# Two quarters of a value projection cut into token pieces: one between attention score steps, one around the transposes of the softmax maxima

## The reference

```
proj = h @ w_in                                   # 1024 -> qc,kc,vc (512 each), qd,kd,vd (768 each)
oc   = stick_breaking(qc, kc, vc)                 # 8 heads of 64
# for each dilation group g in (1, 4, 16), 4 heads of 64:
logits = q k^T / 8 + bias ; masked outside the window
m = max(logits); p = exp(logits - m); den = sum(p)
o_g = p v / den ; lse_g = m + log(den)
od   = sum_g softmax_g(lse_g) * o_g
y    = concat(oc, od) @ w_out
```

## Time and profile before

| | us |
|---|---|
| median of 3 executions | 1382.39 |
| lowest, highest | 1375.46, 1383.12 |
| the profiled execution, its own time | 1371.74 |
| its span, first to last instruction | 1369.9 |
| PE busy in it | 1327.1 (97%) |
| DVE, ACT, POOL busy | 608.6, 466.0, 508.2 |

### The profile page before, as it was taken

One profiled execution on the slowest core, in us unless ns is written; L12 is line 12 of the kernel. 1 busy time (PEld: TensorE's weight loads), 2 busy tenths in 40 slices (PEclk: granted clock), 3 DMA queues, 4 the chain that ended last, 5 costly groups with the idle time before them and its releaser, 6 DMA issues.

```text
span 1369.9 us, 17106 instructions
## 1 busy us (share of the span) xinstructions
PE 1327.1 (97%) x6566; PEld 1107.0 (81%) x6566; DVE 608.6 (44%) x826; ACT 466.0 (34%) x655; POOL 508.2 (37%) x209
## 2 busy tenths in 40 slices
PE   7999999999999999999999999998999999999996
PEld 6778877788888888888888777888888888887885
DVE  5489657767534343401747333367681110100005
ACT  3443353543232322112423433317342322322122
POOL 0343322324453544544343312221154444444444
PEclk9999999999999999999999999989999999999998
DMA  9963437523545465843235311111133322234312
GB/s 335 175 154 100 178 123 139 184 78 123 203 164 204 164 219 179 199 125 106 113 135 184 116 51 62 62 59 56 50 98 95 104 92 92 93 106 138 92 62 62
DMA packets 93539, 173.82 MB, mean 127 GB/s; under 512 B 15735, under 2 KB 61959, under 8 KB 93356
## 3 DMA queue, kind: packets, MB, share of 16 engines
q1 hardware_dynamic: 90344, 169.63, 40.6%
q10 hardware_dynamic: 3140, 3.43, 0.9%
HBM read 170.87 MB, written 4.52 MB: 128 GB/s over the span
## 4 chain that ended last, share of the span: by engine, by line
PE 83%; issue 9%; POOL 4%; DVE 2%; ACT 1%; DMA 0%; POOLq 0%; SPq 0%; DVEq 0%; ACTq 0%
PE ps L1128 15%; PE ps L1129 14%; PE ps L1130 14%; PE ps L1160 5%; PE ps L1162 5%; PE ps L1161 5%; POOL w_lo L697 3%; PE ps L1297 2%; PE ps L1298 2%; PE ps L1299 2%; PE ps L1657 1%; PE ps L1685 1%; PE ps L1311 1%; PE ps L1265 1%; PE ps L1267 1%
## 5 line engine op out<-in xcount | busy, mean ns | idle before, releaser
L697 POOL TENSOR_TENSOR w_lo<-raw,w_hi 128x1024 fp32r<-128x1024 f32 x192 | 476.2, 2485 | 814.4 <-ACT w_hi L751 814.2
L1128 PE MATMUL ps<-h_lo,w_hi 128*128 128x512 f32 (+2 forms) x1064 | 398.0, 374 | 6.9 <-POOL w_lo L697 4.4
L1129 PE MATMUL ps<-h_hi,w_hi 128*128 128x512 f32 (+2 forms) x1064 | 395.1, 371 | 0.0
L1130 PE MATMUL ps<-h_hi,w_lo 128*128 128x512 f32 (+2 forms) x1064 | 394.9, 371 | 0.0
L751 ACT ACTIVATE w_hi<-raw 128x1024 fp32r<-128x1024 f32 x198 | 207.9, 1057 | 480.1 <-DMA raw<-wstream 169.1
L1128 PEld LDWEIGHTS ps<-h_lo,w_hi 128*128 128x128 f32 (+1 forms) x1064 | 201.1, 189 | 46.2 <-issue 7.4
L1130 PEld LDWEIGHTS ps<-h_hi,w_lo 128*128 128x128 f32 (+1 forms) x1064 | 201.2, 189 | 34.7
L1129 PEld LDWEIGHTS ps<-h_hi,w_hi 128*128 128x128 f32 (+1 forms) x1064 | 201.1, 189 | 33.5
L2283 DVE TENSOR_TENSOR tmp<-tmp,ps 128x512 f32<-128x512 f32 x44 | 30.2, 688 | 258.5 <-PE ps L1130 258.5
L1160 PE MATMUL ps<-w_hi,hid_lo 128*128 128x512 f32 x336 | 131.2, 390 | 0.9 <-issue 0.9
L1162 PE MATMUL ps<-w_lo,hid_hi 128*128 128x512 f32 x336 | 130.9, 390 | 0.0
(11 more groups left out here) (287 smaller groups left out, 1621.8 us busy)
## 6 DMA issues: line engine op xcount, KB each, us to landing
raw<-wstream SPq DMA_DIRECT2D x205, 512.0 KB, 4.1
ada_raw<-astream SPq DMA_DIRECT2D x80, 512.0 KB, 4.3
ada_first<-astream SPq DMA_DIRECT2D x16, 256.0 KB, 6.5
ada_first<-astream SPq DMA_DIRECT2D x8, 512.0 KB, 10.7
ln_rows<-row_scratch SPq DMA_DIRECT2D x3, 1024.0 KB, 6.8
skew_scratch<-f_scratch ACTq DMA_DIRECT2D x1, 2304.0 KB
xa<-xT SPq DMA_DIRECT2D x4, 512.0 KB, 8.5
out<-xa SPq DMA_DIRECT2D x3, 512.0 KB, 3.5
```

Of the source, the lines that this page charges most:

```text
L697: nc.gpsimd.tensor_tensor(w_lo[:, slot, :], raw[:, slot % RAW, :], w_hi[:, slot, :].bitcast(F32), ALU.subtract).then_inc(sem("w_lo_ready"), 1)
L1128: pe.matmul(o, w_h, x_l, start=start, stop=False)
L1129: pe.matmul(o, w_h, x_h, start=False, stop=False)
L1130: return pe.matmul(o, w_l, x_h, start=False, stop=stop)
```

## The change

Quarters 2 and 3 of `vd0` no longer stand as two blocks of 24 matmuls. A new function `vd0_piece(i, tb)` does quarter i for one token block, 6 matmuls. The pieces of quarter 2 stand after the score steps 6, 10 and 14 and after the last; of quarter 3, pieces 0 and 1 stand after that, piece 2 between the two turns of the maxima, and piece 3 behind the second. Each piece of the last quarter signals its bank, so the copies out can be taken singly. On DVE the copy of tb 3 moves behind `nm`. On ACT the roundings of `h_hi` come ahead of the two copies of `vd0`, and the slot `OUT[1] + 3` comes behind the first two blocks of exponentials.

```diff
@@ ACT @@
         hi_until(OUT[1] + RING - 1)
-        v_blocks("vd0", v_dst["vd0"])
         for n in range(4):
             e = H_BASE["cat1"] + n
             act.wait_ge(sem("h_tmp_ready"), e + 1)
             nc.scalar.activation(h_hi[:, n, :], staged(n), ACT.Copy).then_inc(sem("h_hi_ready"), 1)
-        hi_until(OUT[1] + RING)
+        v_blocks("vd0", v_dst["vd0"])
...
         dil_exp(0, 0)
         dil_exp(0, 1)
+        hi_until(OUT[1] + RING)
@@ PE @@
-        group("vd0", 2, S, only=(2,))
-
+        def vd0_piece(i, tb):
+
+            s = SLOTS["vd0"][0] + i
+            if tb == 0:
+                slot_waits(s)
+            part, b = ("vd0", tb) if tb < 2 else ("vd0+", tb - 2)
+            o, tokens = ps[:, pair(part) + b, :], slice(tb, S, RES)
+            for kk in range(2):
+                k = 2 * i + kk
+                w = slice(kk * S, (kk + 1) * S)
+                pe.matmul(o, h_lo[:, k, tokens], w_hi[:, s % RING, w], start=False, stop=False)
+                pe.matmul(o, h_hi[:, k, tokens], w_hi[:, s % RING, w], start=False, stop=False)
+                m = pe.matmul(o, h_hi[:, k, tokens], w_lo[:, s % RING, w], start=False, stop=k == KC - 1)
+            if i == 3 and tb < TB - 1:
+                m.then_inc(sem("bank_full"), 1)
+            if tb == TB - 1:
+                m.then_inc(sem("slot_done"), 1)
...
         for s in range(3, 16):
             scores(s)
-        group("vd0", 2, S, only=(3,))
+            if s in (6, 10, 14):
+                vd0_piece(2, s // 4 - 1)
+        vd0_piece(2, 3)
+        vd0_piece(3, 0)
+        vd0_piece(3, 1)
...
         m.then_inc(sem("mx_turned"), 1)
+        vd0_piece(3, 2)
         pe.wait_ge(sem("m_rows_ready"), 1)
...
         m.then_inc(sem("m_turned"), 1)
+        vd0_piece(3, 3)
@@ DVE @@
-        def v_blocks(name):
+        def v_blocks(name, tbs=(1, 3)):
 
-            for tb in (1, 3):
+            for tb in tbs:
...
         i.then_inc(sem("dil_mx"), 1)
-        v_blocks("vd0")
+        v_blocks("vd0", (1,))
...
         V.tensor_scalar(nm, ps[:, 4, 0:32].rearrange("q (a b) -> q a b", a=2), -1.0, None, ALU.mult).then_inc(sem("nm_ready"), 1)
+        v_blocks("vd0", (3,))
```

## The result

| | before | changed |
|---|---|---|
| median of 20 runs, us | 1378.45 | 1371.17 |
| lowest, highest | 1371.33, 1383.95 | 1364.72, 1376.13 |
| the profiled execution, its own time | 1371.74 | 1374.4 |
| its span | 1369.9 | 1372.6 |

The ratio is 0.9944, with a 95% interval of 0.9927 to 0.9961. That is 7.3 us by the medians and 7.7 by the ratio. The forecast was 7.3 us.

What follows compares the result with a forecast made beforehand. PE bounds the kernel (97% busy), but PE and DVE hold each other back in turn from 895.13 to 932.11 us. 8.0 - 0.1 - 0.6 = 7.3 us off 1382.39 gives 1375.1, range 1367 to 1383.

Steps and rivals of the forecast that it cites:

- (a): Front of the scores: without quarter 2 there, the first score follows `sb_av(6)` directly, 5.96 us earlier; last maximum 23.46 later.
- (b): Score steps: pieces fit between them with some 0.6 us margin a block; turn of the maxima 8.0 us sooner (7.5 to 8.1).
- (c): Between the turns: piece (3,2), 1.49 us, fills PE's 1.48 us idle time; cost 0 to 0.2, taken as 0.1.
- (d): Behind the second turn: piece (3,3) and DVE's late bank copy cost 0.1 us at the first transpose, nothing at first product.
- (e): ACT's order: slot `OUT[1] + 3` ahead of the first `pt` copy costs 0.6 us, at most 1.04.
- (f): POOL's `w_lo` of the moved slot, beside DVE's `h_lo` subtractions: taken as 0, bound 1.2 us reaching PE.
- (h): PE's clock: the denser order should keep it at 1.00; gain up to 0.3 us at the first probabilities, left out.
- the rival in which it falls in the score steps: PE's clock drops to 1.2 GHz in the score steps; gain 3.8 us, time 1378.6; chance 0.14.
- ACT and POOL take part of it back: ACT's slot costs the full 1.04 us and POOL's hold the full 2.0; gain 4.9, time 1377.5; chance 0.12.
- The rival of a late start: Something unseen gates the scores until 901; only PE's lateness at the end goes, gain 1.4 us, 1381.0; chance 0.05.
- The slower kernel: Pieces run at half PE clock throughout, turn of the maxima at 932.6; 9 us slower, 1391.4; chance 0.04.
- (g): Queues: SP's loads behind `w_lo` of `OUT[1] + 2` come some 13 us later, user at 947 or later; costs nothing.

Runs made afterwards that it cites:

- four pieces in the loop: Changed kernel, but all four quarter 2 pieces stand between score steps (after 5, 8, 11, 14); output projection 53.93 us behind the first score, 0.8 later.
- slot in the middle of the rounds: Changed kernel, but ACT rounds `OUT[1] + 3` in mid-rounds, not ahead of the first probabilities copy; projection 1.18 us sooner, ratio to before 0.9921.
- quarter 2 alone: Kernel before, with only quarter 2 in pieces between score steps; quarter 3 one block, old ACT and DVE order; projection 4.0 us sooner, ratio 0.9929.
- the two kernels in which only the slot was moved: Changed kernel with ACT's `OUT[1] + 3` mid-rounds, or directly behind the first probabilities copy; output projection 51.95 and 52.56 us behind the first score.
- quarter 3 alone: Kernel before, with only quarter 3 in pieces and the new ACT and DVE order; quarter 2 one block ahead; projection 1.56 us sooner, ratio 0.9944.
- piece ahead: Changed kernel, but piece (3,2) stands ahead of the turn of the maxima, not between the turns; output projection 54.54 us behind the first score, 1.41 later.
- both moves together: Changed kernel with four quarter 2 pieces between score steps and ACT's `OUT[1] + 3` mid-rounds; projection 52.74 us behind the first score, ratio 0.9939.

## Why the prediction was right

- **(a) held exactly.** The first score came 5.96 us sooner, and from it to the last maximum it is 23.47 us, forecast 23.46. No wait took quarter 2's place.
- **(b) held in its size, but the margin was wrong.** I had 8.0 us for the turn; it was 7.53, at the low bound. I had PE done before DVE, with 0.6 us to spare in each block and 0.3 at the end. In the changed kernel a block of PE (15 products and a piece) takes 4.26 to 4.71 us, not 3.94. Part of the 4.71 is still waiting for DVE: steps 8 and 9 start at 915.23 and 915.83, just as DVE ends its reads at 915.17 and 915.77. Such short waits don't show as idle time, since neighbouring matmul records overlap. What counts is the end. From DVE's read of step 8 (919.68) to the turn (928.84) PE took 9.2 us; I had 8.4, and DVE's own work took 8.7. A piece between score steps pays for it in both directions: it is 6 matmuls at 0.235 = 1.41, plus a slow first matmul (917.47 to 917.93, 0.46 us against 0.235) and 0.1 at the change back, 1.73 in all. I had 1.49, with that cost spread over a whole quarter. And the scores behind a piece are dearer too: the last step's three products took 0.87 (923.52 to 924.39), where 0.163 each would be 0.49. The three pieces in a row at the end took 4.45, as I had them. PE was still in piece (3,1) 0.47 us after the last maximum, and the fourth piece in the loop showed that there was no room for it.
- **(c) right, and better than taken**: 0.01 instead of 0.1.
- **(d) nearly right.** From the second turn to the first transpose of the probabilities it is 3.61 us, against 3.00 before and my 3.1. The copy waited for the piece's end, and PE for the copy (0.99 us idle). It cost at most 0.1 further, since the first product can't start ahead of ACT's copy: the kernel with the slot in the middle of the rounds has the same 3.61, its first product 0.9 sooner, and ACT's first copy ends there 0.06 us ahead of that product.
- **(e) right that ACT's slot delays the first product, with two sizes wrong that nearly cancel.** From `nm` to the first product it was 4.47 us before and is 4.82 now (932.48 to 937.30), a loss of 0.35 at this point; against my 0.6. Moving the slot away gained 0.93 there, so the slot itself costs 0.9, nearly its whole 1.04. The other 0.6 comes back from the transposes ahead of the first product. Before the change that product did not wait for ACT, as I had it: ACT's copy ended at 933.47 + 0.57 = 934.04, and the product began at 934.70, behind transposes at 1.2 GHz (1.94 us for the first eight records, 1.06 in the changed kernel). From the first of them to that product it was 2.59 us, and is 1.40 with the slot moved. I had put that at 0.3 and left it out.
- **(f) was wrong by its time, right by its bound.** I placed DVE's subtractions just ahead of POOL's part and just behind it. The pair was held for 2.2 us. Of that 0.25 us reached PE, beyond what (e) cost: the projection's 1.18 less the first product's 0.93.
- **(h) the clock** stayed at 1.00 from 904.90 on, as forecast, and the rival in which it falls in the score steps did not happen. The swinging clock of which the Trainium skill tells (TensorE: Matmul & The Clock Gate, "A second HAM failure mode: psum-queue depth-cycling") is not seen in this loop: 1.00 in all its windows. The clock's own share of the gain is small. Quarter 3 took 6.37 us before at a granted clock of 0.89, quarter 2 5.96 at 1.00: about 0.4 of the 7.5 us at the turn.
- The rival "ACT and POOL take part of it back" did occur in its mechanism, but (e) and (f) cost 1.18 us together, not the 3.04 at which it priced them. The rival of a late start did not: the first score followed `sb_av(6)` directly. The slower kernel needed PE at half clock, which did not come.
- **(g) held.** ACT rounded the slot `OUT[1] + 2` at 926.28, behind piece (2,3), and the projection, at 958.03, did not wait for it.
- **The signs.** One of my own signs of being wrong did come: a DVE subtraction held for more than 2.4 us stands in the rounds (2.85 of the pair's 3.45). It cost PE only 0.25 us. PE's lateness at the turn, 0.47, lay just inside the 0.5 that I allowed. The gap ahead of the first product is ACT's, 0.77 where I had 0.5.

The sum was 7.3 and the stage gave 7.1. Term (b) was 0.5 too high, (c) to (f) together 0.3 too costly. That it comes so close is in part luck: ACT's slot and the held subtraction cost 1.18 where I had 0.6, and the transposes at full clock, which I left out, gave 0.6 back.

## What to carry to other kernels

Dense work that nobody needs early belongs where its engine waits for another, cut into pieces as small as the wait. Price the change-over for every piece and for the short work behind it, not for the block, and count it against the fed engine's slack: here three pieces between the steps were free and the fourth cost 0.8 us. When one step is shifted, look at what the engines behind it, here POOL's half of a weight slot, will now run beside. And when two profiled executions differ by more than the change can explain, measure from the point where the programs part.

## What the runs showed of the hardware

**Spread from the clock.** The programs are the same up to the parting point, and yet the profiled executions reached it at different times. These are the windows of one such stretch for the kernel before and then for the changed one:

```profile
700.00:800.00 100.00, 98.67 (x452) 79.08 (x451) 54.06 (x49) 32.89 (x33) 33.15 (x13) 1.00 0.47 155
```

```profile
700.00:800.00 100.00, 98.67 (x403) 77.16 (x402) 47.59 (x44) 31.80 (x31) 33.86 (x13) 0.90 0.48 153
```

Busy time is the same, but the second execution got 403 matmuls through in it instead of 452, at a mean clock of 0.90. It was at 1.2 GHz for some 20 us of its span between 700 and 780. The executions with the clock at 1.00 there part at 894.4 to 895.7 (before, quarter 2 alone, and the two kernels in which only the slot was moved). Those with some 20 us of low clock part at 904.9 to 906.3 (changed, quarter 3 alone, piece ahead, both moves together). The one with a mean of 0.95 there parts at 900.2 (four pieces in the loop). That spread of 12 us is about that of the 20 runs (12.6 before, 11.4 changed), and larger than the change.

The other executions say the same. For each, the span and its mean granted clock are on record. The product of the two takes off half of all time at 1.2 GHz:

| | executions | span, us | mean clock | span times clock, mean |
|---|---|---|---|---|
| before, run beside the experiments | 24 | 1369.5 to 1381.5 | 0.982 to 0.991 | 1356.7 |
| changed | 20 | 1362.9 to 1374.3 | 0.986 to 0.996 | 1356.4 |
| quarter 2 alone | 4 | 1365.3 to 1371.9 | 0.989 to 0.992 | 1355.4 |
| quarter 3 alone | 4 | 1369.5 to 1378.3 | 0.986 to 0.990 | 1357.4 |
| slot in the middle of the rounds | 4 | 1362.2 to 1370.6 | 0.989 to 0.994 | 1354.8 |
| both moves together | 12 | 1361.7 to 1372.9 | 0.988 to 0.995 | 1355.6 |

The 24 spans of the kernel before lie within 12 us, their products within 2.0. So most of the spread is the clock. In the stage, though, low clock cost little, because PE was seldom the limit in those stretches: there the profiled executions have 13.65 us at 1.2 GHz before and 6.83 with either part alone, and half of that must be added back. As an estimate from these numbers, if every execution has its stage as the profiled one, the gains are 7.2 us for the changed kernel and 4.8, 2.8, 8.8 and 8.0 for the other four, in the order of the table. The stages alone gave 7.1, 4.0, 1.6, 8.3 and 7.5. So the whole runs rank the five kernels as the stages do, within 1.2 us.

Why an execution falls into one or the other I have not tested.

**POOL against DVE.** Of the DVE subtractions with two SBUF inputs that this document follows, three met POOL's work on a slot and ended only after it: 2.39 us against 0.41, 3.45 for a pair against 1.29, and 2.75 against 1.28. POOL waits as well: its 2.4 us became 2.74 and 2.87 where a DVE subtraction had begun before it. It isn't always DVE that is held. In the kernel before, three such subtractions that began right at POOL's start took no longer than alone, and POOL took 3.34 us:

```profile
672.59 1.08 DVE L2174 TENSOR_TENSOR h_lo<-tmp,h_hi 128x256 fp32r<-128x256 f32 x3
...
672.57 3.34 POOL L697 TENSOR_TENSOR w_lo<-raw,w_hi 128x1024 fp32r<-128x1024 f32 x1 [2.21 <-ACT w_hi L751]
```

Nor is a second SBUF tensor needed. This one, from the same kernel, reads one tensor and a column of scalars, and took 2.33 us beside POOL (228.65 to 231.01) where it takes 0.75 alone:

```profile
229.22 2.33 DVE L1828 TENSOR_SCALAR ada_acc<-ada_raw,c_act 128x1024 f32<-128x1024 f32 x1
```

So the rule of (f), that an operation is harmless if it reads one SBUF tensor at most, is too wide. The bias adds, which read PSUM and one SBUF tensor, were not held. Three of them took 1.89 us beside POOL in the changed kernel, 0.63 each, and four took 2.47 away from it, 0.62 each:

```profile
906.16 1.89 DVE L2421 TENSOR_TENSOR lg_dil<-ps,bt 128x512 f32<-128x512 f32 x3 [1.40 <-PE ps L1731]
...
919.00 2.47 DVE L2421 TENSOR_TENSOR lg_dil<-ps,bt 128x512 f32<-128x512 f32 x4
...
904.97 4.67 POOL L697 TENSOR_TENSOR w_lo<-raw,w_hi 128x1024 fp32r<-128x1024 f32 x2 [14.24 <-ACT w_hi L751]
```

For the subtractions that is as the Trainium skill has it (GPSIMD Engine Reference, Specifications), which names DVE instructions with two SBUF inputs among those that contend.
